# A gated group norm moved in among the state-space heads of a two-block transformer kernel

## The chip, the cores and the metric

One Trainium2 chip, one of its cores. The time is the device time of one execution of the whole program in microseconds. The kernel before took 2297.18 us (median of 3 runs, 2294.38 to 2307.04).

## The reference, cut to what matters

The program computes two blocks of two layers each over 256 tokens of width 1024, all in float32. The change is in the second block. One of its layers is, cut:

```python
h = rms_norm(x, norm1_w)
z, xbc, dt_raw, q, k, v = split(h @ w_in)          # z, x: 1024 wide; q: 1024; k, v: 256
xbc = silu(depthwise_conv_centered(xbc, conv_w, conv_b))
y_ssm = ssd_fwd + ssd_bwd + d_skip * xs             # 16 heads of 64, state-space
y_ssm = y_ssm * silu(z)                             # the gate
y_ssm = rms_norm(y_ssm in 2 groups of 512) * w      # one mean of squares per group and token
y_attn = windowed_gqa(q, k, v, sink, band_bias)     # 16 heads of 64
x = x + concat(y_ssm, y_attn) @ w_out
x = x + (silu(conv(h2 @ w_gate)) * (h2 @ w_up)) @ w_down
```

The mean of squares of a group needs all eight heads of that group, and nothing of the other.

## The kernel before

Activations lie transposed: 128 channels on the partitions, 256 tokens in the free dimension, so a width of 1024 is eight tiles of 128x256, and a pair of heads of 64 channels is one tile. Weights stream from memory in chunks of 1 MB through a ring of three (`raw2`). Float32 accuracy comes from splitting: ACT rounds a chunk to `w_hi` (L1664), DVE subtracts to get `w_lo` (L1382), and PE makes three products for each pair of tiles (L1451). So a chunk costs 48 matmuls on PE, two ACTIVATEs and two subtractions. The inputs are split the same way (`u_hi`, `u_lo`; `y_hi`, `y_lo`). Two chunks are held split at a time.

The order of the work is a list, `plan_second` (L1148). Each engine walks the list and issues its part of each step, in order; what crosses engines waits on a counting semaphore. At a chunk's step ACT and DVE first round and subtract the chunk of the next weighted step (`due`, L76), then deal with the step's own result. A step of PE that is held up therefore holds all that comes behind it on PE, and the same for ACT and DVE.

The steps around the change, for each layer:

- `xbc` (six chunks): convolution and silu on DVE and ACT (tanh, in the buffers `cth` and `cacc`).
- then ten chunks interleaved with 23 short steps: `ak2`, `av2`, `aq2` 0 to 3, `z` 0 to 3, in this order, among four `x_turn` and nineteen `ssd` steps. A chunk's projection takes PE about 5.9 us. A `z` chunk is followed by a tanh (L1736, ACT) and a product (L1899, DVE) that leaves 2 silu(z) in `zs`.
- `ssd` i, for the heads: PE spreads the decay of head i (L1600, L1601), DVE makes exponents of it (L1915), ACT takes the exponential (L1743), DVE multiplies by the masked product C B in the next step (L1922), PE multiplies by the tokens three steps later (L1608). After each pair of heads, at even i from 4 to 18, DVE adds the skip term and writes `yT` for that pair (L1926).
- `ssd_gate`: DVE multiplies all eight tiles of `yT` by `zs` and 0.5 in one instruction (L1931); ACT loads the table with log and exp and squares all (L1746, L1747).
- `att2` 0 and 1: the scores of attention heads 0 and 1.
- `ssd_norm`: PE sums the squares of both groups (L1616), ACT takes rsqrt as exp(-0.5 ln) (L1750, L1751), DVE scales eight tiles (L1939), ACT rounds them (L1754), DVE subtracts (L1945).
- `att2` 2 to 18, with the eight `wo2` chunks of the output projection between them. `att2` i holds on PE the scores of head i (L1511), values of head i-3 (L1532), and the turning of the probabilities of head i-2 (L1521); on DVE bias, maximum, division (L1957 to L1969) and the rest of the rounded output (L1976); on ACT two exponentials and two copies. `WO_AFTER` says after which `att2` each `wo2` comes. `wo2` 0 to 3 read `y_hi`, `y_lo`, two tiles each, and 4 to 7 the attention's output. All eight accumulate in the four banks `PB` (the trace's `projected`).
- `rms` 1 and the feed-forward.

Projections take the four `PB` banks in turn (`ROTATED2`, `turn`); scores use banks 0 and 1 of `MB` (`mixed`), turning bank 2, values bank 3, and the state-space pairs banks 2 and 3.

Of the kernel before, what the change touches and what calls it, by code (L numbers as in the profile page):

```python
# [27 lines left out]
P = 128  # L28
# [115 lines left out]
def first_block(nc, ctx, A, hT, k):  # L144
# [966 lines left out]
    with nc.Block() as block:  # L1111

        @block.gpsimd
        def _(pool):
# [24 lines left out]

WO_AFTER = (3, 5, 7, 9, 11, 13, 16, SH + VALUES - 1)  # L1140


COUNT2 = {"rms": 2, "dt": 1, "dt_rows": 1, "xbc": XBC // 2, "dt_columns": 1, "cb": 1, "ak2": 1, "av2": 1, "aq2": 4, "z": 4,
          "x_turn": 4, "ssd": SH + VALUES, "ssd_gate": 1, "att2": SH + VALUES, "ssd_norm": 1, "wo2": 8,
          "wg": FP, "wu": FP, "wd": FP, "add": 1}


def plan_second():  # L1148
    plan = [("rms", 0), ("dt", 0), ("xbc", 4), ("dt_rows", 0), ("xbc", 5), ("dt_columns", 0), ("xbc", 0), ("cb", 0)]
    plan += [("xbc", i) for i in range(1, 4)]  # L1150
    ssd = [("x_turn", i) for i in range(4)] + [("ssd", i) for i in range(SH + VALUES)]
    plan += interleave([("ak2", 0), ("av2", 0)] + [("aq2", i) for i in range(4)] + [("z", i) for i in range(4)], ssd)
    plan += [("ssd_gate", 0), ("att2", 0), ("att2", 1), ("ssd_norm", 0)]

    for i in range(2, SH + VALUES):
        plan += [("att2", i)]
        if i in WO_AFTER:
# [15 lines left out]
HELD2 = [("wd", FP * l + FP - 1) for l in range(DEPTH - 1)] + [("wo2", 8 * l + 7) for l in range(DEPTH)]  # L1173
ROTATED2 = [s for s in PLAN2 if s[0] in WEIGHTED2 and s[0] not in ("wo2", "wd")]
XBC_ORDER = [i for kind, i in plan_second() if kind == "xbc"]


def second_block(nc, ctx, A, hT, k):
# [43 lines left out]
    def place(name, shape, at, dtype=F32):  # L1222
        return nc.alloc_sbuf_tensor_at(name, shape, dtype, offset=area + at * KB)
# [21 lines left out]
    grs = place("grs", [P, SG, T], 8)  # L1245
    y_hi = place("y_hi", [P, KT, T], 10, F32R)
    y_lo = place("y_lo", [P, KT, T], 18, F32R)
    o_hi = place("o2_hi", [P, KT, T], 26, F32R)
# [139 lines left out]
    def taken(step):  # L1388

        kind, N, l, i = local(step)  # L1390
        if kind == "xbc":
            return s_zc, 6 * l + XBC_ORDER.index(i) + 1
        return {"ak2": (s_k, l + 1), "av2": (s_v, l + 1), "aq2": (s_q, N + 1), "z": (s_zs, N + 1),
                "wg": (s_zf, N + 1), "wu": (s_hf, N + 1)}[kind]
# [5 lines left out]
    with nc.Block() as block:  # L1400
# [30 lines left out]
        def _(pe):  # L1431
# [83 lines left out]
            def attention_turn(l, n):  # L1515
                U = SH * l + n
                pe.wait_ge(s_an, U + 1)
                if U:
                    pe.wait_ge(s_pt, U)
                for b in range(4):  # L1520
                    m = pe.transpose(MB[2][:, b * P:(b + 1) * P], S[:, n % ABUF, b // 2, b % 2 * P:(b % 2 + 1) * P], ident[:])  # L1521
                m.then_inc(s_at, 1)
# [13 lines left out]
            for step in PLAN2:  # L1536
# [54 lines left out]
                elif kind == "ssd":  # L1591
# [10 lines left out]
                    if i >= VALUES:  # L1602
# [8 lines left out]
                        m.then_inc(s_y, 1)  # L1611
                elif kind == "ssd_norm":
                    pe.wait_ge(s_ysq, l + 1)
                    for g in range(SG):
                        for n in range(4):
                            m = pe.matmul(PB[0][:, g * T:(g + 1) * T], ones_g[:], sq[:, 4 * g + n, :],  # L1616
                                          start=n == 0, stop=n == 3)
                    m.then_inc(s_yvar, 1)
# [9 lines left out]
                elif kind == "wo2":  # L1628
                    if i in (0, 2):
                        pe.wait_ge(s_yn, 2 * l + i // 2 + 1)  # L1630
                    if i >= 4:
# [11 lines left out]
        def _(act):  # L1643
# [22 lines left out]
            def halves(ap):  # L1666
                return ap.rearrange("p (a t) -> p a t", a=2)

            for step in PLAN2:
# [62 lines left out]
                elif kind == "z":  # L1732
                    b = result(step)
                    if N >= 2:
                        act.wait_ge(s_zs, N - 1)
# [4 lines left out]
                elif kind == "ssd":  # L1740
                    if i < SH:
                        act.wait_ge(s_ex, SH * l + i + 1)
                        act.activation(W[:, i % ABUF, :], W[:, i % ABUF, :], ACT.Exp).then_inc(s_ee, 1)  # L1743
                elif kind == "ssd_gate":
                    act.wait_ge(s_yg, l + 1)
                    act.preload_act_table_set(LOG_EXP)  # L1746
                    act.activation(sq[:], yT[:], ACT.Square).then_inc(s_ysq, 1)  # L1747
                elif kind == "ssd_norm":
                    act.wait_ge(s_yvar, l + 1)
                    link(act.activation(grs[:], halves(PB[0][:]), ACT.Ln, bias=eps[:, 0:1]))  # L1750
                    act.activation(grs[:], grs[:], ACT.Exp, scale=-0.5).then_inc(s_yrs, 1)  # L1751
# [37 lines left out]
        def _(dve):  # L1789
# [37 lines left out]
            for step in PLAN2:  # L1827
# [81 lines left out]
                elif kind == "ssd":  # L1909
# [13 lines left out]
                    if i > VALUES and i % 2 == 0:  # L1923
# [3 lines left out]
                                                 in1=MB[2 + pair % 2][:, 0:T], op0=ALU.mult, op1=ALU.add).then_inc(s_yT, 1)  # L1927
                elif kind == "ssd_gate":
                    dve.wait_ge(s_yT, KT * l + KT)
                    dve.wait_ge(s_zs, 4 * l + 4)  # L1930
                    dve.scalar_tensor_tensor(out=yT[:].rearrange("p a t -> p (a t)"), in0=zs[:].rearrange("p a t -> p (a t)"),  # L1931
                                             scalar=0.5, in1=yT[:].rearrange("p a t -> p (a t)"),
                                             op0=ALU.mult, op1=ALU.mult).then_inc(s_yg, 1)
                elif kind == "ssd_norm":
                    dve.wait_ge(s_yg, l + 1)
                    dve.wait_ge(s_yrs, l + 1)
                    for n in range(2):
                        for kt in range(4 * n, 4 * n + 4):
                            ins = dve.scalar_tensor_tensor(out=yT[:, kt, :], in0=yT[:, kt, :], scalar=column(l, V2_SN + kt),  # L1939
                                                           in1=grs[:, n, :], op0=ALU.mult, op1=ALU.mult)  # L1940
                        ins.then_inc(s_yf, 1)
                    for n in range(2):
                        quad = slice(4 * n, 4 * n + 4)
                        dve.wait_ge(s_yh, 2 * l + n + 1)
                        dve.tensor_tensor(y_lo[:, quad, :], yT[:, quad, :], y_hi[:, quad, :].bitcast(F32),  # L1945
                                          ALU.subtract).then_inc(s_yn, 1)
# [377 lines left out]
```

## Time and profile before

| | |
|---|---|
| runs | 2307.04, 2294.38, 2297.18 us |
| profiled execution | 2307.46 us, its span 2305.7 us |
| PE busy | 2057.5 us, 89% |
| DVE busy | 1556.6 us, 68% |
| ACT busy | 989.3 us, 43% |
| mean granted clock of PE | 0.949 |

The profile is of one execution. Busy time of an engine counts the time in which at least one of its instructions ran. The granted clock is the share of TensorE's full speed, 2.4 GHz, that the chip granted; at the lower level, 1.2 GHz, it is 0.5. A timeline row has the start, the duration, the engine and line, the operation, what it writes and reads, and in brackets how long the engine was idle before and what ended that. PE's matmuls overlap, so the start to start distance (some 0.12 us for 128x256) is what counts, and not the duration. A float32 matmul that isn't split leaves two records. For steps that stand in both layers the rows are those of the first; its heads run from 1403 to 1489 us and its attention to 1600 us, those of the second from 1889 to 1974 and to 2085 us.

### The profile page before, as it was taken

To read this page: it belongs to the slowest core of one execution; us is meant where nothing else is said; L and a number is where in the kernel's file an instruction comes from. 1 tells how busy PE (TensorE), PEld (TensorE's weight loads), DVE (VectorE), ACT (ScalarE), POOL (GpSimd) and SP (SyncE) were. 2 spreads that over 40 slices of the span, in tenths; PEclk is the share of its full clock that TensorE was granted. 3 is DMA by queue.
4 is the path that set the end of the run, shared out by engine and by line. 5 is a ranking of instruction groups with operands and counts; after the bars stand their busy time and mean duration, and the time that the engine had idled before them with its cause. 6 is when DMAs were issued, how large, how long until landed. Compare 5 with 4: busy or idle time off the path is not lost. (4 is left out here: it accounts for less than half of the span.)

```text
span 2305.7 us, 37153 instructions
## 1 busy us (share of the span) xinstructions
PE 2057.5 (89%) x15578; PEld 1927.2 (84%) x15578; DVE 1556.6 (68%) x2612; ACT 989.3 (43%) x1424; POOL 16.5 (1%) x36
## 2 busy tenths in 40 slices
PE   2799999999988999999999588987999789897996
PEld 1798888989988988899999567776999678687996
DVE  5687767677668876766755368765666588665664
ACT  1453355444444534544444224444444324444442
POOL 0000000000010000000000000000000000000000
PEclk7899999999999999999999889999999899899998
DMA  5455533548744554344555134211555232123551
GB/s 214 165 188 196 190 122 146 183 158 304 259 158 142 201 189 165 132 162 165 212 209 183 70 132 144 92 67 63 194 191 189 74 132 106 62 85 132 198 194 63
DMA packets 52627, 358.98 MB, mean 156 GB/s; under 512 B 6107, under 2 KB 8763, under 8 KB 9836
## 3 DMA queue, kind: packets, MB, share of 16 engines
q1 hardware_dynamic: 52268, 356.51, 43.3%
q8 instruction: 123, 2.02, 0.4%
q14 instruction: 44, 0.36, 0.0%
q10 hardware_dynamic: 192, 0.10, 0.0%
HBM read 355.40 MB, written 1.08 MB: 155 GB/s over the span
## 5 line engine op out<-in xcount | busy, mean ns | idle before, releaser
L362 DVE TENSOR_TENSOR w_lo<-raw,w_hi 128x1024 fp32r<-128x1024 f32 x340 | 410.0, 1229 | 242.9 <-ACT w_hi L637 241.4
L417 PE MATMUL projected<-u_hi,w_hi 128*128 128x256 f32 x1728 | 492.1, 285 | 46.3 <-DVE w_lo L362 38.3
L637 ACT ACTIVATE w_hi<-raw 128x1024 fp32r<-128x1024 f32 x340 | 351.8, 1054 | 386.8 <-PE projected L417 311.7
L417 PE MATMUL projected<-u_lo,w_hi 128*128 128x256 f32 x1728 | 485.7, 281 | 0.0
L417 PE MATMUL projected<-u_hi,w_lo 128*128 128x256 f32 x1728 | 485.1, 281 | 0.0
L417 PEld LDWEIGHTS projected<-u_hi,w_hi 128*128 128x128 f32 x1728 | 332.3, 192 | 53.8 <-DVE w_lo L362 39.2
L1382 DVE TENSOR_TENSOR w_lo<-raw,w_hi 128x1024 fp32r<-128x1024 f32 x204 | 246.0, 1223 | 143.7 <-ACT w_hi L1664 143.5
L417 PEld LDWEIGHTS projected<-u_lo,w_hi 128*128 128x128 f32 x1728 | 330.7, 191 | 0.3
L417 PEld LDWEIGHTS projected<-u_hi,w_lo 128*128 128x128 f32 x1728 | 330.4, 191 | 0.0
L1451 PE MATMUL projected<-u_hi,w_hi 128*128 128x256 f32 x992 | 281.4, 284 | 25.9 <-DVE w_lo L1382 25.9
L1451 PE MATMUL projected<-u_lo,w_hi 128*128 128x256 f32 x992 | 279.1, 281 | 0.0
L1451 PE MATMUL projected<-u_hi,w_lo 128*128 128x256 f32 x992 | 278.9, 281 | 0.0
L1664 ACT ACTIVATE w_hi<-raw 128x1024 fp32r<-128x1024 f32 x204 | 210.9, 1054 | 157.3 <-PE projected L1451 138.9
L1451 PEld LDWEIGHTS projected<-u_hi,w_hi 128*128 128x128 f32 x992 | 189.7, 191 | 32.7 <-issue 23.4
L1451 PEld LDWEIGHTS projected<-u_lo,w_hi 128*128 128x128 f32 x992 | 191.0, 193 | 0.0
L1451 PEld LDWEIGHTS projected<-u_hi,w_lo 128*128 128x128 f32 x992 | 189.1, 191 | 0.0
L417 PE MATMUL mixed<-hid_hi,w_hi 128*128 128x256 f32 x352 | 98.2, 279 | 1.0 <-DVE w_lo L362 1.0
L417 PE MATMUL mixed<-hid_lo,w_hi 128*128 128x256 f32 x352 | 98.0, 279 | 0.0
L417 PE MATMUL mixed<-hid_hi,w_lo 128*128 128x256 f32 x352 | 98.0, 279 | 0.0
L1451 PE MATMUL mixed<-hid_hi,w_hi 128*128 128x256 f32 x352 | 98.0, 278 | 0.0
L1451 PE MATMUL mixed<-hid_lo,w_hi 128*128 128x256 f32 x352 | 98.0, 278 | 0.0
L1451 PE MATMUL mixed<-hid_hi,w_lo 128*128 128x256 f32 x352 | 98.0, 278 | 0.0
(355 smaller groups left out, 4132.7 us busy)
## 6 DMA issues: line engine op xcount, KB each, us to landing
raw<-in_stream_dram SPq DMA_DIRECT2D x324, 1024.0 KB, 4.9
w_mod<-in_first_ada_dram SPq DMA_DIRECT2D x8, 1024.0 KB, 13.8
band<-bias_rows SPq DMA_DIRECT2D x1, 3072.0 KB, 13.0
x<-in_xT_dram SPq DMA_DIRECT2D x1, 1024.0 KB
out_dram<-f_sq SPq DMA_DIRECT2D x2, 512.0 KB, 2.6
tri<-in_tri_dram SPq DMA_DIRECT2D x2, 384.0 KB, 4.5
c<-in_c_dram SPq DMA_DIRECT2D x1, 512.0 KB
mask<-in_mask_dram SPq DMA_DIRECT2D x1, 384.0 KB, 3.8
```

Of the source, the lines that this page charges most:

```text
L362: eng.tensor_tensor(part(w_lo, step, half), raw_half(step, half), part(w_hi, step, half).bitcast(F32), ALU.subtract).then_inc(s_lo_pool if ...
L417: m = pe.matmul(out, a, b, start=start and n == 0, stop=stop and n == 2, **kw)
L637: act.activation(part(w_hi, step, half), raw_half(step, half), ACT.Copy).then_inc(s_hi, 1)
L1382: eng.tensor_tensor(part(w_lo, step, half), raw_half(step, half), part(w_hi, step, half).bitcast(F32), ALU.subtract).then_inc(s_lo_pool if ...
L1451: m = pe.matmul(out, a, b, start=start and n == 0, stop=stop and n == 2, **kw)
L1664: act.activation(part(w_hi, CHUNKS2[n], half), raw_half(CHUNKS2[n], half), ACT.Copy).then_inc(s_hi, 1)
```

## The change

- The norm's two parts become one step kind, `group_norm` 0 and 1, one for each group.
- Gate and square move into `ssd`, by pair: DVE gates the tile as soon as `yT` of the pair is there (even i from 4 to 18), ACT squares it in the same step.
- `group_norm` 0 stands behind `ssd` 11; its sum goes to a bank of the rotation. `group_norm` 1 stands behind `att2` 1, with its sum in `MB[2]`, the bank of the turned probabilities; the first turning waits until it was read. The table with log and exp is loaded in `group_norm` 0 only.
- Rounding and subtraction go by two tiles, with a count for each of the four `wo2` chunks that read them.
- The chunks among the heads come in the order `z` 0 to 3, `ak2`, `av2`, `aq2` 0 to 3. `z` 0 and 1 wait on ACT for the last convolution, whose buffers they use.
- `wo2` 0 comes behind `group_norm` 1, and `WO_AFTER` is (1, 3, 5, 7, 9, 12, 15, 18).
- `y_hi` lies over `zs` and `y_lo` over `yT`.

```diff
-WO_AFTER = (3, 5, 7, 9, 11, 13, 16, SH + VALUES - 1)
+WO_AFTER = (1, 3, 5, 7, 9, 12, 15, SH + VALUES - 1)
...
-    plan += interleave([("ak2", 0), ("av2", 0)] + [("aq2", i) for i in range(4)] + [("z", i) for i in range(4)], ssd)
-    plan += [("ssd_gate", 0), ("att2", 0), ("att2", 1), ("ssd_norm", 0)]
+    plan += interleave([("z", i) for i in range(4)] + [("ak2", 0), ("av2", 0)] + [("aq2", i) for i in range(4)], ssd)
+    plan.insert(plan.index(("ssd", 11)) + 1, ("group_norm", 0))
+    plan += [("att2", 0), ("att2", 1), ("group_norm", 1), ("wo2", 0)]
...
-    y_hi = place("y_hi", [P, KT, T], 10, F32R)
-    y_lo = place("y_lo", [P, KT, T], 18, F32R)
+    y_hi = place("y_hi", [P, KT, T], 58, F32R)
+    y_lo = place("y_lo", [P, KT, T], 50, F32R)
...
             def attention_turn(l, n):
                 U = SH * l + n
                 pe.wait_ge(s_an, U + 1)
+                if n == 0:
+                    pe.wait_ge(s_yrs, SG * l + SG)
...
-                elif kind == "ssd_norm":
-                    pe.wait_ge(s_ysq, l + 1)
-                    for g in range(SG):
-                        for n in range(4):
-                            m = pe.matmul(PB[0][:, g * T:(g + 1) * T], ones_g[:], sq[:, 4 * g + n, :],
-                                          start=n == 0, stop=n == 3)
+                elif kind == "group_norm":
+                    out = bank(step) if i == 0 else MB[2]
+                    pe.wait_ge(s_ysq, 4 * N + 4)
+                    for n in range(4):
+                        m = pe.matmul(out[:, 0:T], ones_g[:], sq[:, 4 * i + n, :], start=n == 0, stop=n == 3)
                     m.then_inc(s_yvar, 1)
...
-                    if i in (0, 2):
-                        pe.wait_ge(s_yn, 2 * l + i // 2 + 1)
+                    if i < 4:
+                        pe.wait_ge(s_yn, 4 * l + i + 1)
...
                 elif kind == "z":
                     b = result(step)
+                    if i < 2:
+                        act.wait_ge(s_xbc, 6 * l + 6)
...
-                elif kind == "ssd_gate":
-                    act.wait_ge(s_yg, l + 1)
-                    act.preload_act_table_set(LOG_EXP)
-                    act.activation(sq[:], yT[:], ACT.Square).then_inc(s_ysq, 1)
...
+                    if i > VALUES and i % 2 == 0:
+                        pair = (i - 4) // 2
+                        act.wait_ge(s_yg, KT * l + pair + 1)
+                        act.activation(sq[:, pair, :], yT[:, pair, :], ACT.Square).then_inc(s_ysq, 1)
+                elif kind == "group_norm":
+                    act.wait_ge(s_yvar, N + 1)
+                    if i == 0:
+                        act.preload_act_table_set(LOG_EXP)
+                    out = PB[turn(step)] if i == 0 else MB[2]
+                    link(act.activation(grs[:, i, :], out[:, 0:T], ACT.Ln, bias=eps[:, 0:1]))
+                    act.activation(grs[:, i, :], grs[:, i, :], ACT.Exp, scale=-0.5).then_inc(s_yrs, 1)
                     for n in range(2):
-                        act.wait_ge(s_yf, 2 * l + n + 1)
-                        act.activation(y_hi[:, 4 * n:4 * n + 4, :], yT[:, 4 * n:4 * n + 4, :], ACT.Copy)\
-                           .then_inc(s_yh, 1)
+                        pair = slice(4 * i + 2 * n, 4 * i + 2 * n + 2)
+                        act.wait_ge(s_yf, 2 * N + n + 1)
+                        act.activation(y_hi[:, pair, :], yT[:, pair, :], ACT.Copy).then_inc(s_yh, 1)
...
-                elif kind == "ssd_gate":
-                    dve.wait_ge(s_yT, KT * l + KT)
-                    dve.wait_ge(s_zs, 4 * l + 4)
-                    dve.scalar_tensor_tensor(out=yT[:].rearrange("p a t -> p (a t)"), in0=zs[:].rearrange("p a t -> p (a t)"),
-                                             scalar=0.5, in1=yT[:].rearrange("p a t -> p (a t)"),
-                                             op0=ALU.mult, op1=ALU.mult).then_inc(s_yg, 1)
...
+                        dve.wait_ge(s_yT, KT * l + pair + 1)
+                        dve.wait_ge(s_zs, 4 * l + pair // 2 + 1)
+                        dve.scalar_tensor_tensor(out=yT[:, pair, :], in0=zs[:, pair, :], scalar=0.5, in1=yT[:, pair, :],
+                                                 op0=ALU.mult, op1=ALU.mult).then_inc(s_yg, 1)
```

On DVE `group_norm` i scales the four tiles of its group (two by two), and subtracts them two by two, each counted in `s_yn`.

## Rows read from the trace of the kernel before

**Rows 1.** The page, part 1: busy us, share of the span, instructions of each engine.

```profile
PE 2057.5 (89%) x15578; PEld 1927.2 (84%) x15578; DVE 1556.6 (68%) x2612; ACT 989.3 (43%) x1424; POOL 16.5 (1%) x36
```

**Rows 2.** Stretches: length, busy us of each engine, granted clock, DMA share, GB/s.

```profile
1489.00:1524.90 35.90, 25.08 (x129) 20.54 (x129) 24.50 (x59) 16.07 (x37) 0.00 (x0) 0.81 0.11 38
1974.00:2009.60 35.60, 24.78 (x129) 20.33 (x129) 24.50 (x59) 16.06 (x37) 0.00 (x0) 0.81 0.11 38
1524.90:1536.40 11.50, 10.85 (x84) 9.39 (x82) 7.86 (x22) 5.51 (x15) 0.00 (x0) 1.00 0.27 93
1427.50:1489.00 61.50, 61.37 (x423) 49.31 (x422) 47.62 (x85) 25.74 (x31) 0.00 (x0) 1.00 0.29 100
```

**Rows 3.** Waits of PE from 1489.0 to 1524.9: us, times, longest.

```profile
PE mixed L1532 <- ACT PT L1763: 3.7, 1, 3.7
```

**Rows 4.** Timeline of PE, 1489 to 1525: start, duration, line, what; idle before.

```profile
1489.60 1.14 PE L1511 MATMUL mixed<-kT,qT 64*128 64x256 f32 x8 [0.57 <-DVE yT L1926]
...
1495.15 5.41 PE L1616 MATMUL projected<-sq,ones_m 128*128 128x256 f32 x16 [4.41 <-ACT sq L1747]
...
1511.17 0.56 PE L1451 MATMUL projected<-y_hi,w_hi 128*128 128x256 f32 x1
...
1524.91 0.37 PE L1451 MATMUL projected<-y_hi,w_hi 128*128 128x256 f32 x1
```

**Rows 5.** Timeline of DVE, 1489 to 1511.

```profile
1489.58 2.29 DVE L1931 SCALAR_TENSOR_TENSOR yT<-zs,yT 128x2048 f32<-128x2048 f32 x1
1491.79 0.68 DVE L1957 TENSOR_TENSOR S<-mixed,band 128x512 f32<-128x512 f32 x1
...
1493.57 0.68 DVE L1957 TENSOR_TENSOR S<-mixed,band 128x512 f32<-128x512 f32 x1
...
1502.04 3.26 DVE L1939 SCALAR_TENSOR_TENSOR yT<-yT,vec,grs 128x256 f32<-128x256 f32 x8 [4.83 <-ACT grs L1751]
...
1507.57 0.68 DVE L1957 TENSOR_TENSOR S<-mixed,band 128x512 f32<-128x512 f32 x1
...
1510.27 0.68 DVE L1957 TENSOR_TENSOR S<-mixed,band 128x512 f32<-128x512 f32 x1
```

**Rows 6.** Timeline of ACT, the same stretch.

```profile
1491.89 1.28 ACT L1746 ACT_TABLE_LOAD   x1 [6.02 <-DVE yT L1931]
1493.18 1.91 ACT L1747 ACTIVATE sq<-yT 128x2048 f32<-128x2048 f32 x1
1495.00 0.19 ACT L1772 ACTIVATE es<-es 128x2 f32<-128x2 f32 x1
...
1496.08 0.19 ACT L1772 ACTIVATE es<-es 128x2 f32<-128x2 f32 x1
```

**Rows 7.** Timeline of DVE among the state-space heads.

```profile
1435.47 1.39 DVE L1915 TENSOR_SCALAR W<-mixed,cols 128x256 f32<-128x256 f32 x4 [1.83 <-PE mixed L1608]
...
1453.63 0.69 DVE L1899 SCALAR_TENSOR_TENSOR zs<-cth,projected 128x512 f32<-128x512 f32 x1 [0.52 <-ACT cth L1736]
1455.17 1.39 DVE L1915 TENSOR_SCALAR W<-mixed,cols 128x256 f32<-128x256 f32 x4 [0.85 <-PE mixed L1608]
```

**Rows 8.** Groups by line and shape, 1386 to 1625: busy us, mean ns | idle before.

```profile
L1939 DVE SCALAR_TENSOR_TENSOR yT<-yT,vec,grs 128x256 f32<-128x256 f32 x8 | 3.3, 481 | 4.8 <-ACT grs L1751 4.8
...
L1684 ACT ACTIVATE rstd<-lnv 128x256 f32<-128x256 f32 x1 | 0.4, 416 | 0.0
...
L1542 PE MATMUL mixed<-sqn,ones_d 128*128 128x256 f32 x16 | 3.7, 386 | 1.4 <-ACT sqn L1679 1.4
```

**Rows 9.** Stretches with their clock, and PE's row after a long idle.

```profile
1594.60:1600.40 5.80, 5.71 (x48) 5.51 (x48) 0.03 (x1) 0.81 (x1) 0.00 (x0) 1.00 0.00 0
1511.10:1519.20 8.10, 8.10 (x51) 7.97 (x51) 4.18 (x10) 3.68 (x8) 0.00 (x0) 0.71 0.17 43
...
1878.00:1885.00 7.00, 6.97 (x48) 6.93 (x48) 6.42 (x15) 0.55 (x2) 0.00 (x0) 0.79 0.44 150
...
1878.03 0.55 PE L1451 MATMUL projected<-u_hi,w_hi 128*128 128x256 f32 x1 [4.27 <-DVE w_lo L1382]
```

More of the change, by code:

```diff
@@ L1137 @@
 V2_END = V2_SINK + AH
-WO_AFTER = (3, 5, 7, 9, 11, 13, 16, SH + VALUES - 1)
+WO_AFTER = (1, 3, 5, 7, 9, 12, 15, SH + VALUES - 1)
 COUNT2 = {"rms": 2, "dt": 1, "dt_rows": 1, "xbc": XBC // 2, "dt_columns": 1, "cb": 1, "ak2": 1, "av2": 1, "aq2": 4, "z": 4,
-          "x_turn": 4, "ssd": SH + VALUES, "ssd_gate": 1, "att2": SH + VALUES, "ssd_norm": 1, "wo2": 8,
+          "x_turn": 4, "ssd": SH + VALUES, "group_norm": 2, "att2": SH + VALUES, "wo2": 8,
           "wg": FP, "wu": FP, "wd": FP, "add": 1}
@@ L1173 @@
 HELD2 = [("wd", FP * l + FP - 1) for l in range(DEPTH - 1)] + [("wo2", 8 * l + 7) for l in range(DEPTH)]
-ROTATED2 = [s for s in PLAN2 if s[0] in WEIGHTED2 and s[0] not in ("wo2", "wd")]
+ROTATED2 = [s for s in PLAN2 if s[0] in WEIGHTED2 and s[0] not in ("wo2", "wd") or s[0] == "group_norm" and s[1] % SG == 0]
 XBC_ORDER = [i for kind, i in plan_second() if kind == "xbc"]
@@ L1392, in taken @@
             return s_zc, 6 * l + XBC_ORDER.index(i) + 1
-        return {"ak2": (s_k, l + 1), "av2": (s_v, l + 1), "aq2": (s_q, N + 1), "z": (s_zs, N + 1),
+        return {"group_norm": (s_yrs, N + 1), "ak2": (s_k, l + 1), "av2": (s_v, l + 1), "aq2": (s_q, N + 1), "z": (s_zs, N + 1),
                 "wg": (s_zf, N + 1), "wu": (s_hf, N + 1)}[kind]
@@ L1743, in _ @@
                         act.activation(W[:, i % ABUF, :], W[:, i % ABUF, :], ACT.Exp).then_inc(s_ee, 1)
-                elif kind == "ssd_gate":
-                    act.wait_ge(s_yg, l + 1)
-                    act.preload_act_table_set(LOG_EXP)
-                    act.activation(sq[:], yT[:], ACT.Square).then_inc(s_ysq, 1)
[L1748 to L1751, printed above, removed]
+                    if i > VALUES and i % 2 == 0:
[9 more added lines that the diff above has]
+                    act.activation(grs[:, i, :], grs[:, i, :], ACT.Exp, scale=-0.5).then_inc(s_yrs, 1)
                     for n in range(2):
-                        act.wait_ge(s_yf, 2 * l + n + 1)
-                        act.activation(y_hi[:, 4 * n:4 * n + 4, :], yT[:, 4 * n:4 * n + 4, :], ACT.Copy)\
-                           .then_inc(s_yh, 1)
+                        pair = slice(4 * i + 2 * n, 4 * i + 2 * n + 2)
+                        act.wait_ge(s_yf, 2 * N + n + 1)
+                        act.activation(y_hi[:, pair, :], yT[:, pair, :], ACT.Copy).then_inc(s_yh, 1)
                 elif kind == "att2":
@@ L1927, in _ @@
                                                  in1=MB[2 + pair % 2][:, 0:T], op0=ALU.mult, op1=ALU.add).then_inc(s_yT, 1)
-                elif kind == "ssd_gate":
-                    dve.wait_ge(s_yT, KT * l + KT)
-                    dve.wait_ge(s_zs, 4 * l + 4)
-                    dve.scalar_tensor_tensor(out=yT[:].rearrange("p a t -> p (a t)"), in0=zs[:].rearrange("p a t -> p (a t)"),
-                                             scalar=0.5, in1=yT[:].rearrange("p a t -> p (a t)"),
-                                             op0=ALU.mult, op1=ALU.mult).then_inc(s_yg, 1)
-                elif kind == "ssd_norm":
-                    dve.wait_ge(s_yg, l + 1)
-                    dve.wait_ge(s_yrs, l + 1)
+                        dve.wait_ge(s_yT, KT * l + pair + 1)
+                        dve.wait_ge(s_zs, 4 * l + pair // 2 + 1)
+                        dve.scalar_tensor_tensor(out=yT[:, pair, :], in0=zs[:, pair, :], scalar=0.5, in1=yT[:, pair, :],
+                                                 op0=ALU.mult, op1=ALU.mult).then_inc(s_yg, 1)
+                elif kind == "group_norm":
+                    dve.wait_ge(s_yg, 4 * N + 4)
+                    dve.wait_ge(s_yrs, N + 1)
                     for n in range(2):
-                        for kt in range(4 * n, 4 * n + 4):
+                        for kt in range(4 * i + 2 * n, 4 * i + 2 * n + 2):
                             ins = dve.scalar_tensor_tensor(out=yT[:, kt, :], in0=yT[:, kt, :], scalar=column(l, V2_SN + kt),
-                                                           in1=grs[:, n, :], op0=ALU.mult, op1=ALU.mult)
+                                                           in1=grs[:, i, :], op0=ALU.mult, op1=ALU.mult)
                         ins.then_inc(s_yf, 1)
                     for n in range(2):
-                        quad = slice(4 * n, 4 * n + 4)
-                        dve.wait_ge(s_yh, 2 * l + n + 1)
-                        dve.tensor_tensor(y_lo[:, quad, :], yT[:, quad, :], y_hi[:, quad, :].bitcast(F32),
+                        pair = slice(4 * i + 2 * n, 4 * i + 2 * n + 2)
+                        dve.wait_ge(s_yh, 2 * N + n + 1)
+                        dve.tensor_tensor(y_lo[:, pair, :], yT[:, pair, :], y_hi[:, pair, :].bitcast(F32),
                                           ALU.subtract).then_inc(s_yn, 1)
```

## The prediction

> **What bounds the kernel now.** I read the busy table first: PE is busy 89% of the span, DVE 68% [rows 1]. So an edit pays where PE stands idle, or where it closes a gap after which PE runs slow. The windows by stage say where that is. Among the state-space heads PE is busy for 61.37 of 61.50 us at clock 1.00. From 1489.0 to 1524.9, where the heads end, the norm runs and the attention starts, it is busy for 25.08 of 35.90 us at clock 0.81; the second layer repeats it with 24.78 of 35.60 [rows 2]. The reader should see in these four lines that the change aims at the one stage of its neighbourhood in which PE waits.
>
> The timelines tell why. PE has issued the scores of two attention heads at 1489.60 and then waits 4.41 us for the squares [rows 4]: DVE gates all eight tiles in one 2.29 us instruction [rows 5], then ACT loads a table (1.28) and squares all of them (1.91) [rows 6]. PE sums the squares in 5.41 us, at the low clock. DVE cannot start to normalise before 1502.04, and holds the third score block until 1507.57 [rows 5], for which PE waits 3.7 us with the attention [rows 3]. wo2 0 starts at 1511.17, wo2 1 at 1524.91 [rows 4]. wo2 0 takes 8.0 us at clock 0.71, where a chunk of 48 matmuls at clock 1.00 takes 5.71 [rows 9]. Idle is 35.90 - 25.08 = 10.8 us; the low clock costs 2.3 there and 5.41 - 3.72 = 1.7 in the sum of squares, going by the equal sum of 16 at L1542 [rows 8]. Together 14.8 us per layer is to be had.
>
> From wo2 1 on, the section runs in periods of 11.5 us: one wo2 chunk (5.7) and two attention heads (5.8), of which PE is busy 10.85 [rows 2]. There DVE has 3.6 us to spare per period.
>
> **The heads, with z first.** z 0 and z 1 take the places of ak2 and av2. The weights are of one size, 1 MB each, in the same ring, so SP's queue is as before. z 1 may start on its first half, where av2 waited for both; that gives PE about 1.2 us, but DVE now has four z products of 0.69 [rows 7] among x_turn and the first heads, and the first values product already waits for DVE there. I take +0.3 us (bounds -1.2 and +1.5). ACT's new wait of z 0 for the last convolution is met before its weights are rounded; queued behind it are the roundings for z 2, which PE wants 6 us later.
>
> **Gate and square by pair.** Each of eight pairs gets a gate on DVE, by the same shape 0.48 [rows 8] (2.29 in one piece goes), and a square on ACT of 0.42, going by an ACTIVATE of that size [rows 8]. Behind each square on ACT stands the rounding of the next chunk, and behind that DVE's subtraction: with the handovers it all comes 1.4 us later per pair. DVE now waits for PE after it, 1.83 us before an ordinary pair [rows 7], so it fits. In the later pairs the slack is only 0.85, but a z product (0.69 and the 0.52 waited for it) stood there and is gone [rows 7]. Cost on PE 0; if the cover fails, up to 0.5 per pair. The end of the heads: gate and square of pair 7 are 1.0 us after the last product instead of 6.1.
>
> **First group's norm among the heads.** PE goes into group_norm 0 right behind step 11. The gate of pair 3 ends on DVE about 1.2 us after PE is there, the square 0.5 later: a wait of 1.75 us, where behind it on PE stands the projection aq2 1, and for that all of ACT and DVE. Then 4 matmuls, half of 3.72 [rows 8]: 1.86. The rest lies beside the projection: table load 1.28 [rows 6], Ln and Exp 0.47 and 0.42, two pairs scaled (4 x 0.41 from 3.26 for 8 [rows 5]), rounded and subtracted, some 5.3 us in all. ACT's rounding for aq2 2 comes 5.5 us later than now and DVE is through with it some 8 us after the projection began; PE wants it after 10 (5.9 of projection, 4.2 of two heads). So the cover holds by about 2 us. Lower bound of the whole step: 1.9, the matmuls alone; upper: 1.9 + 4.4, the wait for squares as it is now [rows 4].
>
> So the heads end 0.3 + 1.75 + 1.86 = 3.9 us later, less 0.1 for the z product that stood before the last head: 3.8.
>
> **From the last head to wo2 1**, counted from the end of the last values product. Scores of two heads 0.6 to 1.7, as now. Squares are ready at 1.5, sum of the second group 1.75 to 3.6. wo2 0 follows at once, as the first group is long normalised: 3.6 to 9.3, at full clock, and its weights were rounded before. In this time DVE and ACT do the rest. DVE: scores 0 and 1 take 1.78 each [rows 5], from 1.6 to 5.2, the division of head 0 until 6.2. ACT: exponentials, 1.1 per head [rows 6], until 6.4, then Ln and Exp until 7.4. DVE scales, ACT rounds, DVE subtracts until 10.4; the weights of wo2 1 are rounded and subtracted by 13.1 (2.36 on DVE). Then DVE takes score block 2 and the division of head 1, 2.7 together [rows 5]: 15.9. PE meanwhile runs scores 2, turn 0, scores 3, values 0 until 13.4 and waits 2.6 us for turn 1. The new wait of turn 0 for the group's reciprocal root was met at 7.4. wo2 1 starts at 16.4.
>
> Now it starts at 35.9 [rows 2], but behind two more heads, worth 5.8; so the gain is 35.9 - 16.4 - 5.8 = 13.7. Less 3.8: 9.9 us. For the second layer, with 35.6, it is 9.6.
>
> **Rest of the attention.** wo2 5 and 6 stand behind groups of three heads, and three heads are left before wo2 7. PE's stalls of 0.65 per odd head: one fewer in the middle, one of 1.4 instead of 0.7 at the end. Taken as 0 (bounds -0.5, +1.5 per layer).
>
> Sum: 9.9 + 9.6 = 19.5 us. The profiled execution took 2307.46 us (span 2305.7) and would take 2288.0. Its time lies above the median of the three runs, 2297.18; from this I get 2277.7.
>
> **The clock in the new gaps.** After 4.27 us without a matmul the stretch 1878 to 1885 has clock 0.79 [rows 9]. The Trainium skill ("TensorE: Matmul & The Clock Gate", section "HAM oscillation — how this bites in real kernels") says that a loop whose bursts are separated by waits goes back to half rate each time and pays for warming up each time. By it the 2.6 us wait ahead of turn 1 would hand wo2 1 the price that wo2 0 has now; the trace has an idle stretch only longer than this one to show for it.
>
> On the table load the Trainium skill ("ScalarE: Activation LUTs", section "What ACT_TABLE_LOAD costs") adds a drain to the load, 2.66 us in all. The row differs: the Square starts 0.01 us after the 1.28 us load [rows 6]. By the page group_norm 0 would end 1.4 us later, and most of the 2 us of cover would be gone.
>
> **Rivals.**
> 1. The clock falls in the gap at turn 1 (or the gaps around group_norm 0 come longer). Mechanism in rows: 2.3 us for a slow chunk of wo2 [rows 9], and 1.5 more of waiting at group_norm 0. Per layer 9.8 - 3.8 = 6.0, so -12: 2285. For it: 4.27 us of idle do it, and DVE's chain in the attention is long. Against: 2.6 is much shorter. Chance 0.20.
> 2. More is closed than I count: the wait at turn 1 vanishes because the weights are rounded earlier, and group_norm 0 finds its squares ready. Then 9.8 + 2.6 + 1.75 = 14.1 per layer, -28: 2269. For: the full 14.8 is what the rows offer. Against: DVE's order is fixed. Chance 0.12.
> 3. No gain: with wo2 earlier, the attention is paced by its own DVE and ACT chain, and what PE saves ahead it waits for later. It takes 1.4 us on each of seven periods. Against: 3.6 us of DVE slack per period [rows 2]. Time 2297. Chance 0.08.
> 4. Slower: the pair's chain (gate, square in front of the rounding on ACT, rounding, subtraction) delays the next head's exponents beyond the slack, in every pair. Place: DVE's first instruction of a pair; from 1.83 us of delay on it costs PE one for one [rows 7]. To pay back 9.8 per layer it must overshoot by 1.4 on each of seven pairs; at 4 us of chain, it overshoots by 2.2, 15 per layer against 9.8: +11, 2308. Against: 0.48 and 0.42 are measured shapes. Chance 0.04.
> That the edit does not do what it says would be wo2 0 waiting all the same, since it needs squares of pair 3 through y_lo; they are 30 us old by then, so I leave it out.
>
> **Numbers.** My forecast has 0.56. A measurement of this kernel tells 0.5% (11.5 us) from no change. Rival 1 lies at this edge; three quarters of it count as faster. Faster 0.56 + 0.12 + 0.14 = 0.82, same 0.14, slower 0.04. The forecast alone spans 2271 to 2284 (2 to 3 us each way per layer). The range takes in rivals 1 and 2 and the spread of the medians: 2266 to 2290.
>
> **What would show it.** The stretch from the last L1608 to the second wo2 chunk, 35.9 now, should be 16 to 17 us. The sum of squares should appear twice per layer, 8 records each; PE's wait before the first 1 to 2.5 us. wo2 0 should take 5.7 us at clock 1.00. PE in the heads should have no wait but that one. The table load should stand among the heads. The prediction is wrong if PE waits for W or w_lo among the heads in several pairs, if PE waits over 4 us at turn 1, or if the period after wo2 1 exceeds 11.5.

## The result and the profile after

The changed kernel takes 2285.28 us (median of 7 runs, 2277.00 to 2292.26), the kernel before 2300.94 us on the same chips (7 runs, 2294.38 to 2308.85). The ratio is 0.9925, with a 95% interval from 0.9897 to 0.9952, so 17 us are gained, with an uncertainty of 6. The profiled execution took 2287.97 us.

```profile
span 2286.2 us, 37218 instructions
...
PE 2045.6 (89%) x15578; PEld 1918.2 (84%) x15578; DVE 1558.6 (68%) x2630; ACT 993.1 (43%) x1446; POOL 16.5 (1%) x36
```

PE is busy for 12 us less than before in the first part of the page, with the same 15578 matmuls [rows 1]. Of these, 7.6 us lie in the stages that the change touches (4.1 and 3.5, by windows): there slow matmuls have gone as well as gaps. The rest comes from stretches in which both kernels have the same code.

The windows of the first layer after: the heads, from the first x_turn to the end of the last values product (PE's product of the last head with its tokens, L1611); from there to wo2 1; and wo2 1 itself (columns as in [rows 2]).

```profile
1397.80:1488.10 90.30, 87.30 (x616) 72.29 (x616) 74.47 (x132) 44.91 (x60) 0.00 (x0) 1.00 0.32 110
1488.10:1504.50 16.40, 12.76 (x89) 10.81 (x89) 13.57 (x34) 8.40 (x23) 0.00 (x0) 1.00 0.23 84
1504.50:1511.80 7.30, 7.30 (x51) 7.17 (x49) 4.38 (x11) 3.68 (x8) 0.00 (x0) 0.77 0.23 65
```

The 35.9 us of [rows 2] have become 16.4, at clock 1.00, and PE is busy in 12.76 of them. But wo2 1 runs at clock 0.77. The timeline of PE, same layer:

```profile
1457.53 0.89 PE L1619 MATMUL projected<-sq,ones_m 128*128 128x256 f32 x3 [1.79 <-ACT sq L1751]
...
1488.65 1.14 PE L1512 MATMUL mixed<-kT,qT 64*128 64x256 f32 x8 [0.57 <-DVE yT L1933]
1489.73 1.99 PE L1619 MATMUL mixed<-sq,ones_m 128*128 128x256 f32 x8
1491.37 0.47 PE L1452 MATMUL projected<-y_hi,w_hi 128*128 128x256 f32 x1
...
1500.38 1.09 PE L1535 MATMUL mixed<-PT,vA 128*64 128x128 f32 x8 [0.50 <-ACT PT L1770]
1504.05 0.66 PE L1524 MATMUL mixed<-ident,S 128*128 128x128 f32 x4 [2.58 <-DVE S L1974]
1504.46 0.37 PE L1452 MATMUL projected<-y_hi,w_hi 128*128 128x256 f32 x1
...
1511.71 0.48 PE L1512 MATMUL mixed<-kT,qT 64*128 64x256 f32 x1
```

The answers to [rows 4], in order: the first sum stands among the heads with a wait of 1.79 us; the second follows the scores at once and wo2 0 follows it at 1491.37, 3.3 us after the last values product (22.2 before). Ahead of turn 1, the turning of the probabilities of head 1, PE waits 2.58 us, and wo2 1 then takes 7.3 us. DVE's timeline says why PE waits:

```profile
1488.63 0.42 DVE L1937 SCALAR_TENSOR_TENSOR yT<-zs,yT 128x256 f32<-128x256 f32 x1
1489.82 0.69 DVE L1962 TENSOR_TENSOR S<-mixed,band 128x512 f32<-128x512 f32 x1 [0.76 <-PE mixed L1512]
...
1495.61 1.67 DVE L1944 SCALAR_TENSOR_TENSOR yT<-yT,vec,grs 128x256 f32<-128x256 f32 x4 [1.21 <-ACT grs L1758]
1497.20 1.47 DVE L1950 TENSOR_TENSOR y_lo<-yT,y_hi 128x512 fp32r<-128x512 f32 x2
1498.92 2.36 DVE L1383 TENSOR_TENSOR w_lo<-raw,w_hi 128x1024 fp32r<-128x1024 f32 x2 [0.25 <-ACT w_hi L1666]
1501.20 0.68 DVE L1962 TENSOR_TENSOR S<-mixed,band 128x512 f32<-128x512 f32 x1
...
1503.37 0.62 DVE L1974 TENSOR_SCALAR S<-S,den 128x256 f32<-128x256 f32 x2
```

Scores, then the second group's scaling (1495.61) and subtraction (1497.20), the weights of wo2 1 (1498.92), and only then score block 2 (1501.20) and the division of head 1 (1503.37), done at 1503.99. Turn 1 follows at 1504.05. Among the heads, ACT has the first group's norm:

```profile
1456.97 0.42 ACT L1751 ACTIVATE sq<-yT 128x256 f32<-128x256 f32 x1 [0.88 <-DVE yT L1937]
...
1459.52 1.28 ACT L1755 ACT_TABLE_LOAD   x1 [0.40 <-PE projected L1619]
1460.82 0.47 ACT L1757 ACTIVATE grs<-projected,eps 128x256 f32<-128x256 f32 x1
1461.32 0.42 ACT L1758 ACTIVATE grs<-grs 128x256 f32<-128x256 f32 x1
```

For a ledger I measure one stage in each layer: from the first x_turn matmul to the end of wo2 7. It took 198.9 and 199.0 us before and 189.9 and 190.7 after: 17.3 us together, which is the measured gain. The spans of the two profiles differ by 19.5 us. The rest comes from stretches with the same code: up to the first x_turn the profile of after is 3.7 us shorter, between the two stages 1.9 longer, behind the second 0.4 shorter.

### The profile page after: what moved, and what is told of

Its sections match the earlier page's. It is cut to its first block and busy times, and to the rows that moved or that the text cites. A ratio compares the mean times of both kernels' runs of the same rounds, so it can differ in the third digit from the quotient of the medians.

```text
span 2286.2 us, 37218 instructions
## 1 busy us (share of the span) xinstructions
PE 2045.6 (89%) x15578; PEld 1918.2 (84%) x15578; DVE 1558.6 (68%) x2630; ACT 993.1 (43%) x1446; POOL 16.5 (1%) x36
## 5 line engine op out<-in xcount | busy, mean ns | idle before, releaser
L1452 PE MATMUL projected<-u_hi,w_hi 128*128 128x256 f32 x992 | 282.3, 285 | 26.4 <-DVE w_lo L1383 26.4
```

The lines of the kernel that those rows point to most:

```text
L1452: m = pe.matmul(out, a, b, start=start and n == 0, stop=stop and n == 2, **kw)
```

## Experiments

Starts of wo2 chunks are counted from the end of the last values product; "stage" is the stretch of the ledger, in the first and the second layer. Each kernel was profiled once and the changed one twice. The ratios to before have intervals of 6 to 10 us to either side, more than most steps between neighbours. So the steps are read from the stages and the waits in them; the ratios show a gain against before from the third kernel on, and little order among the kernels.

**A ladder from before to after.** The first three kernels go from one to the other in steps; the fourth takes the early group away from the full change.

*z first alone*: the kernel before, with

```diff
-    plan += interleave([("ak2", 0), ("av2", 0)] + [("aq2", i) ...] + [("z", i) ...], ssd)
+    plan += interleave([("z", i) ...] + [("ak2", 0), ("av2", 0)] + [("aq2", i) ...], ssd)
```

and the wait of the first two z chunks.

> The kernel before with one edit: z chunks first, ak2, av2 and aq2 behind them. Measured on the stage from the first x_turn matmul to the last wo2 matmul: before 198.9 and 199.0 us in the two layers, after the change 189.9 and 190.7. My theory: the gain comes from PE's waits around the norm, which this edit leaves alone; it only takes the z product from in front of the last head (0.6 to 1.0 us). Stage 198 us, run 1 to 3 us below before. Rival (the order of the chunks is what helps, since gate and table load no longer collide with tanh): stage 194 or less, run 8 us or more below before.

Measured: stage 199.0 and 198.8; 2300.48 us, ratio to before 1.0011 (0.9982 to 1.0041). The first values product comes 0.9 us earlier, the last only 0.4 to 0.6, and wo2 0 0.3 later after it. The order of the chunks gives nothing by itself that these numbers show; the 1 us that I expected was too much.

*Gate and square by pair, norms at the end*: the change without

```diff
-    plan.insert(plan.index(("ssd", 11)) + 1, ("group_norm", 0))
-    plan += [("att2", 0), ("att2", 1), ("group_norm", 1), ("wo2", 0)]
+    plan += [("att2", 0), ("att2", 1), ("group_norm", 0), ("group_norm", 1)]
```

and with the old WO_AFTER.

> The change with both group norms behind att2 1 and the wo2 chunks at their old places (after att2 3, 5, 7, 9, 11, 13, 16, 18): so z first and gate and square by pair, nothing else. My theory: the squares are ready 1.5 us after the last values product instead of 6.1, but the table load and both groups' scaling still stand ahead of the third score block; wo2 0 starts about 18 us after the last values product (22.1 before), stage about 194. Rival (early gates and squares are the whole gain): wo2 0 at 12 or less, stage 190 as after.

Measured: heads 87.1 and 86.9 (87.2 and 87.0 with z first alone), wo2 0 starts at 18.8, stage 195.4 and 195.1 (I expected 194); ratio 0.9975 (0.9943 to 1.0008). PE has no wait for the last head's product here. PE's waits in the 36 us behind the last values product (us, times, longest) have one large entry, the reciprocal root of the second group, for which the bank of the turning is held:

```profile
PE mixed L1523 <- ACT grs L1757: 5.8, 1, 5.8
```

*First group among the heads, wo2 at the old places*: the change with the old WO_AFTER and no wo2 0 behind group_norm 1.

```diff
-WO_AFTER = (1, 3, 5, 7, 9, 12, 15, SH + VALUES - 1)
+WO_AFTER = (3, 5, 7, 9, 11, 13, 16, SH + VALUES - 1)
-    plan += [("att2", 0), ("att2", 1), ("group_norm", 1), ("wo2", 0)]
+    plan += [("att2", 0), ("att2", 1), ("group_norm", 1)]
```

> The change with the wo2 chunks at their old places only; the first group's norm is among the heads. My theory: wo2 0 starts 13.6 us after the last values product (DVE has one group less ahead of the attention), but the heads take 3.6 us longer, so the stage is about 193, 1 us better than without the early group, and 3 us worse than the full change, since PE has nothing to fill the wait for DVE. Rival (the early first group is what brings the gain): stage 190, as after. The other rival (it costs more in the heads than it gives): stage 195 or more.

Measured: wo2 0 at 14.1, heads 90.5 and 90.2, stage 192.9 and 192.9; ratio 0.9959 (0.9930 to 0.9989). The early group is worth 2.6 and 2.2 us at this step, where I had expected 1. The same wait has halved, and wo2 0 behind it takes 7.1 us instead of 8.1:

```profile
PE mixed L1524 <- ACT grs L1758: 2.8, 1, 2.8
```

*Norms late, wo2 0 right behind*: the full change but for group_norm 0, which stands just ahead of group_norm 1.

```diff
-    plan.insert(plan.index(("ssd", 11)) + 1, ("group_norm", 0))
-    plan += [("att2", 0), ("att2", 1), ("group_norm", 1), ("wo2", 0)]
+    plan += [("att2", 0), ("att2", 1), ("group_norm", 0), ("group_norm", 1), ("wo2", 0)]
```

> The change with group_norm 0 moved from behind ssd 11 to just ahead of group_norm 1, wo2 0 still right behind. My theory: the heads get 3.6 us shorter, wo2 0 starts at about 11 us after the last values product instead of 3.3 and at the low clock, wo2 1 at 21 to 22.5 instead of 16.4; stage 192 to 193, 2.5 us per layer worse than the change. Rival (the wait and the sum inside the heads cost as much as they bring): stage 190, same as after. If the early group were the main thing, the stage would be 195 or more.

Measured: heads 87.5 and 87.1, wo2 0 at 11.3, wo2 1 at 23.8, stage 193.0 and 192.7; ratio 0.9944 (0.9916 to 0.9973). That is 3.1 and 2.0 worse than the change; wo2 1 comes later than the 21 to 22.5 that I expected. Now PE waits ahead of wo2 0, for the first group's rest:

```profile
PE projected L1451 <- DVE y_lo L1949: 5.9, 1, 5.9
```

So in the first layer: 0.1 lost by the order, 3.5 gained by gating and squaring in pairs, 2.6 by the early group, 3.0 by wo2 0 in the gap and the other new places of wo2. In the second: 0.2, 3.7, 2.2 and 2.2 gained. And the early group, once wo2 0 fills the gap, is worth 3.1 and 2.0. No single part is the change. I had expected 1, 4, 1 and 3.

**The waits that are left.** Each of the next kernels takes one wait out of the changed kernel. The recorded expectations call them n1 to n6.

*First norm one projection later* (n1): group_norm 0 behind ssd 13.

```diff
-    plan.insert(plan.index(("ssd", 11)) + 1, ("group_norm", 0))
+    plan.insert(plan.index(("ssd", 13)) + 1, ("group_norm", 0))
```

> The change with group_norm 0 behind ssd 13 instead of ssd 11, so one projection later on PE. My theory: PE's 1.8 us wait for the squares of pair 3 is a matter of place only; it goes, and nothing takes its stead: stage 188.1 and 188.9 (after: 189.9 and 190.7), run 3 to 4 us below after. Rival (ACT and DVE are too late for the last chunk then, as the norm's 5 us chain now stands nearer to the end of the heads): PE waits for w_lo or W among the last heads and the stage stays at 190.

Measured: stage 190.4 and 190.7, not shorter; ratio 0.9901 (0.9869 to 0.9934). The wait for the squares is gone, and another stands in its place, 1.0 us (1.4 in the second layer) for DVE's product of the last head (L1611; PE's waits in the heads):

```profile
PE mixed L1592 <- DVE xbc L1891: 1.1, 1, 1.1
PE mixed L1611 <- DVE W L1929: 1.0, 1, 1.0
PE mixed L1603 <- DVE W L1922: 0.8, 1, 0.8
```

So the rival holds, for 1.0 and 1.4 of the missing 1.8 us. The rest lies in chunks that took 5.9 to 6.0 us where they took 5.7 to 5.8 in the profile of after, with no wait in them (see the last section).

*Second group scaled later* (n2): scaling, rounding and subtraction of group_norm 1 become a step of their own behind att2 3.

```diff
+        if i == 3:
+            plan += [("group_scale", 0)]
```

> The change with the second group's scaling, rounding and subtraction (3 us on DVE) taken out of group_norm 1 and put behind att2 3; the sum, Ln and Exp stay. My theory: PE's 2.6 us wait for turn 1 is DVE's queue, in which the second group stands in front of score block 2; it goes, and with it the low clock in which wo2 1 took 7.3 us instead of 5.7: wo2 1 starts 13.7 us after the last values product (16.4 in after) and takes 5.7; stage 4.2 shorter, 185.7 and 186.5, run 8 us below after. Rival (the attention's own chain of scores, exponentials and division is the limit there): wait for turn 1 stays above 1.5, stage 188 or more. Rival on the clock (the low clock of wo2 1 has nothing to do with the wait): wo2 1 still takes 7.3.

Measured: wo2 1 at 13.95 in both layers (16.38), stage 187.0 and 189.2, where I expected 185.7 and 186.5; ratio 0.9882 (0.9837 to 0.9926). Timelines of DVE and then of PE:

```profile
1495.54 0.68 DVE L1968 TENSOR_TENSOR S<-mixed,band 128x512 f32<-128x512 f32 x1
...
1497.71 0.62 DVE L1980 TENSOR_SCALAR S<-S,den 128x256 f32<-128x256 f32 x2
...
1500.94 1.67 DVE L1950 SCALAR_TENSOR_TENSOR yT<-yT,vec,grs 128x256 f32<-128x256 f32 x4
1502.53 1.47 DVE L1956 TENSOR_TENSOR y_lo<-yT,y_hi 128x512 fp32r<-128x512 f32 x2
1504.26 2.36 DVE L1385 TENSOR_TENSOR w_lo<-raw,w_hi 128x1024 fp32r<-128x1024 f32 x2 [0.26 <-ACT w_hi L1668]
1506.54 0.68 DVE L1968 TENSOR_TENSOR S<-mixed,band 128x512 f32<-128x512 f32 x1
...
1498.38 0.65 PE L1526 MATMUL mixed<-ident,S 128*128 128x128 f32 x4 [0.52 <-DVE S L1980]
...
1509.80 1.06 PE L1537 MATMUL mixed<-PT,vA 128*64 128x128 f32 x8 [1.59 <-DVE o_lo L1987]
```

and the window of wo2 1:

```profile
1498.80:1504.40 5.60, 5.60 (x51) 5.49 (x48) 5.07 (x16) 4.19 (x10) 0.00 (x0) 1.00 0.16 69
```

The wait ahead of turn 1 is 0.52, wo2 1 takes 5.7 us at clock 1.00. So the wait was DVE's queue, and the low clock came with the wait: both rivals fall. The other profiles bear it out. With 2.58 us ahead of turn 1 (the change, its second execution, the kernels with the norm behind ssd 13 and with the tail edit) wo2 1 takes 7.3 to 7.4 us, in all eight cases; with 0.5 to 0.7 (this kernel and the last three) 5.7 to 5.9, in all eight. But 1.59 us are now waited for o_lo where the changed kernel waits 0.65: the scaling stands in front of score block 4 instead. wo2 2 starts 3.1 us earlier, not 4.2. In the second layer the last chunk, wo2 7, took 7.32 us instead of 5.73, at the low clock, behind waits no longer than in the other profiles (see the last section).

*Tail* (n3): wo2 6 one place later.

```diff
-WO_AFTER = (1, 3, 5, 7, 9, 12, 15, SH + VALUES - 1)
+WO_AFTER = (1, 3, 5, 7, 9, 12, 16, SH + VALUES - 1)
```

> The change with wo2 6 behind att2 16 instead of 15. My theory: the 1.5 us wait ahead of the values of head 14 gets covered by the chunk again: stage 0.8 us shorter, run 1.6 below after, hard to see in the time. Rival: the stall moves and the stage stays.

Measured: wo2 7 starts at 93.4 and 93.3 (93.9 and 94.1), stage 189.6 and 189.2; ratio 0.9902 (0.9864 to 0.9940). The stall of 1.5 us is gone, and 0.5 to 0.8 us of it is to be seen at wo2 7. In the stage it is 0.3 and 1.5, as the heads differ from profile to profile too.

*All three* (n4): the edits of n1, n2 and n3 together.

```diff
-WO_AFTER = (1, 3, 5, 7, 9, 12, 15, SH + VALUES - 1)
+WO_AFTER = (1, 3, 5, 7, 9, 12, 16, SH + VALUES - 1)
-    plan.insert(plan.index(("ssd", 11)) + 1, ("group_norm", 0))
+    plan.insert(plan.index(("ssd", 13)) + 1, ("group_norm", 0))
+        if i == 3:
+            plan += [("group_scale", 0)]
```

> The three edits of n1, n2 and n3 together. If they are independent waits on PE, the stage is 1.8 + 4.2 + 0.8 = 6.8 us shorter than after in each layer: 183.1 and 183.9, run about 13.5 us below after and 31 below before. If one of them only uncovers another wait, it is less: the rival says that DVE becomes the limit between the last head and wo2 1, and gives 186 or more.

Measured: stage 186.3 and 186.7, ratio 0.9861 (0.9823 to 0.9898). The three waits are not independent: 3 us of the expected 6.8 are missing. What is there is the gain of the second and third edit; the first gives nothing again, with a wait of 1.0 and 1.4 us for the last head's product. The rival has the number right but not the place: wo2 1 starts at 13.96 as with the second edit alone.

**Two better places, and the change once more.** The changed kernel ran again beside the two:

> The changed kernel itself, unedited, beside the two versions below. What repeats in a second execution is the kernel's, and what doesn't is the chip's. My theory: wo2 0 and wo2 1 start 3.3 and 16.4 us after the last values product again, wo2 1 takes 7.2 to 7.3 us, the wait ahead of the first sum is 1.8, and the stage from x_turn to wo2 7 is within 1 us of 190.3. The feed-forward, whose code the change leaves alone, took 195.5 us in some profiles and 202 to 203 in others with no wait of PE in either; it will be one of these two. Rival: the stage differs by 2 us or more, and then the terms of my sum cannot be read from single profiles.

Measured: wo2 0 at 3.29 and wo2 1 at 16.38 and 16.39, a wait of 1.78 for the first sum, 2.58 for turn 1, wo2 1 7.32 and 7.42 us; stage 190.7 and 190.8; ratio 0.9906 (0.9879 to 0.9933). The waits repeat to 0.01 us, the stage to 0.8, and the first feed-forward took 196.2 us where it had taken 203.4.

*Behind a projection* (n5, against the kernel with all three):

```diff
-    plan.insert(plan.index(("ssd", 13)) + 1, ("group_norm", 0))
+    plan.insert(plan.index(("aq2", 1)) + 1, ("group_norm", 0))
```

> The scaling after att2 3 and wo2 6 behind att2 16 as in n4, but group_norm 0 straight behind the projection aq2 1 instead of behind ssd 13. In n1, behind ssd 13, PE's wait for the squares was gone and 1.0 us of waiting for the products of DVE had come at the end of the heads. My theory: that was the chain of 5 us standing too near the end; 4.2 us earlier it is covered at both ends: no wait at the sum, none but the 0.6 before the attention at the end, stage 184.6 to 185.6 (n4: 186.3 and 186.7), as 1.8 is saved against the change instead of 0.8. Rival (DVE's total among the heads is what lacks, wherever the norm stands): a wait of about 1 us turns up at the end or at a values product again, stage 186 or more.

Measured: stage 186.4 and 187.1, ratio 0.9874 (0.9844 to 0.9904), as the rival has it. No wait at the sum, and the one at the end is there as before (1.15, in the second layer 1.52). PE:

```profile
1464.78 1.89 PE L1621 MATMUL projected<-sq,ones_m 128*128 128x256 f32 x8
...
1490.09 0.86 PE L1613 MATMUL mixed<-W,xtok_fwd 128*64 128x256 f32 x4 [1.15 <-DVE W L1933]
```

DVE ahead of it:

```profile
1482.71 0.47 DVE L1937 SCALAR_TENSOR_TENSOR yT<-xbc,vec,mixed 128x256 f32<-128x256 f32 x1
1483.22 0.42 DVE L1941 SCALAR_TENSOR_TENSOR yT<-zs,yT 128x256 f32<-128x256 f32 x1
1483.56 1.38 DVE L1926 TENSOR_SCALAR W<-mixed,cols 128x256 f32<-128x256 f32 x4
...
1486.81 2.36 DVE L1385 TENSOR_TENSOR w_lo<-raw,w_hi 128x1024 fp32r<-128x1024 f32 x2 [0.99 <-ACT w_hi L1668]
1489.09 0.95 DVE L1933 TENSOR_TENSOR W<-W,cbm 128x768 f32<-128x768 f32 x1
```

Here my theory falls: in both places DVE comes to the last head's product (1489.09) only behind its last weights (1486.81), and those stand behind pair 5's two instructions, 0.9 us of them, and ACT's square and rounding. In the changed kernel PE comes 1.0 us later to the same place (1.9 in the second layer) and finds the product done, by 0.06 and 0.3 us. So the wait for the squares cost less than it looked, because a wait of over 1 us stood behind it. Gate and square alone don't make that wait: with the norms late (the second and fourth kernel of the ladder) the same instructions stand there and PE doesn't wait for the last product. It comes only with the first group's norm among the heads, which gives DVE 3.1 us of scaling and subtraction and PE a sum of 1.6. And it is the heads as a whole that don't yield: in all nine profiles with the early group they take 90.2 to 90.9 us, in whichever of the three places it stands. That DVE's total sets this is argued from these numbers, and no run takes work off DVE there.

*Scaling in two halves*, behind att2 3 and 4 (n6, against the kernel with the norm behind a projection):

```diff
+        if i in (3, 4):
+            plan += [("group_scale", i - 3)]
```

> As n5, but the second group is scaled in two parts, a pair after att2 3 and a pair after att2 4. In n2 and n4 PE's wait at turn 1 was gone, and 1.4 to 1.6 us of waiting for o_lo had come after wo2 1, where the changed kernel waits 0.65: DVE's queue, one step later. My theory: with half the scaling in front of score block 4 this wait falls to about 0.7, stage 0.8 shorter than n5, run 1 to 2 us. Rival (DVE is short of time between the heads and wo2 2 as a whole): the wait moves to wo2 2, which needs both pairs, and the stage stays.

Measured: the wait for o_lo is 0.80, wo2 2 starts at 25.6 (26.4), stage 185.6 and 185.3, so 0.7 and 1.8 shorter, as expected or better; 2271.02 us (6 runs), ratio to before 0.9864 (0.9836 to 0.9893); the changed kernel beside it took 2279.23 us. The wait of 1.15 at the last head is still there. By the stage this is the version to keep: it is 13.2 and 13.7 us shorter than before, where the change gives 9.0 and 8.3. By the time alone it can't be told from the kernel with all three edits (ratio 0.9861).

## Why the prediction was right

The time came out 17.3 us below before by the ratio, against 19.5, and where the gain was to come from is where it came from. The time itself, 2285.28 us, is 7.6 above the forecast of 2277.7 and outside the 2271 to 2284 that the forecast alone spans; it lies in the range because the range takes in rival 1 and the spread of the medians. Half of the 7.6 (3.8) is that the kernel before has 2300.94 over seven runs, where I had 2297.18 from three. That the profiled execution took 2287.97 where I had 2288.0 is luck: 2.2 of the 19.5 us between the two profiles lie in stretches with the same code. Part of the sum is luck too: in the first layer the clock took 1.6 us that I had left out and the rest of the attention 0.4, and the heads gave back 1.05.

- **The gap** (35.9 to 16.4 by the working): 16.38, in both layers and in two executions. Each item stands in the trace where the working had it, the squares 1.4 us after the last product, DVE's order, turn 1 at the end.
- **The heads** (3.8 longer): 2.75 and 3.3. The wait was 1.79 against 1.75, the sum 1.6 instead of 1.86, and z first gave 0.4 to 0.6 where I charged 0.3. The wait for the squares is not the only one, as I had said it would be: with z first PE waits 0.8 us at the first heads for DVE's W, and the 1.4 us for w_lo that stood ahead of them are down to 0.3. The cover of 2 us behind the first sum was 1.6: the weights of aq2 2 were ready at 1467.53, and PE took them at 1469.08.
- **Gate and square cost PE nothing**: true, by the ladder. The heads take 87.1 and 86.9 us with them and 87.2 and 87.0 without (z first alone). The reason I gave covers the pairs; I did not look at the last head, where DVE's product was done 0.6 us before PE wanted it without them and 0.3 with them. There the work of the early group is felt as soon as the norm stands at another place (1.0 to 1.5 us, norm behind ssd 13 or behind aq2 1), and in the changed kernel it was hidden behind the wait for the squares. It has something of my fourth rival, at one place instead of seven and not through gate and square alone.
- **The clock**, in the first rival with 2.3 us per layer: it happened, behind a gap of 2.58 us, with 1.6 (7.32 against 5.71; in the second layer 1.4, against 5.90). The half of rival 1 on more waiting at group_norm 0 did not happen. This is the largest term that the forecast lacked, and my reason against it, that 2.6 us is much shorter than 4.27, was wrong. The kernel with the second group scaled later shows the wait as the cause: with 0.5 instead of 2.6 us of waiting the chunk takes 5.7. The trace agrees in kind with what the Trainium skill says ("TensorE: Matmul & The Clock Gate", section "HAM oscillation — how this bites in real kernels"), a burst behind a wait that starts at half rate; the waits of its example are longer than 2.58 us, so by it alone the term could not be sized. The 1.79 us gap among the heads left the projection behind it at 5.8 and 6.0.
- **Rest of the attention as 0**: 0.4 us lost, the stall of 1.5 at the values of head 14 (the tail experiment).
- **Table load**: Ln starts 0.02 us after the load of 1.28 (1459.52 and 1460.82 above). The drain that the Trainium skill adds ("ScalarE: Activation LUTs", section "What ACT_TABLE_LOAD costs") is not to be seen; the measurement decides.
- **The chances**: three quarters of rival 1's 0.20 are 0.15, and not the 0.14 that I added up.

First layer: -13.7 (the gap, two heads deducted) + 2.75 + 1.6 + 0.4 = -8.95, which is the stage's difference. The rivals "no gain" and "slower" are refuted by the period behind wo2 2, 11.47 us as before, and by the waits among the heads, of which none stands behind a pair's gate and square. As for the second rival, its 14.1 us per layer are nearly to be had, but by another order of DVE's work: the last kernel gets 13.2 and 13.7.

## What to carry to other kernels

Walk the instruction queues of all engines item by item through a gap that is to be closed: the order on DVE decided here to 0.1 us what remained. After it, look at who stands just behind the wait that you remove, since a second, shorter wait can be hidden there. And give a gap of PE that is left a second price, that of a slow chunk behind it: here 2.58 us of waiting cost 1.4 to 1.6 more.

## What the runs showed of the hardware

**PE has two paces at the same granted clock.** In windows of 50 us with PE busy throughout, in the first feed-forward, the kernel before and the one with z first (same instructions there) had:

```profile
1700.00:1750.00 50.00, 50.00 (x427) 50.00 (x426) 31.73 (x42) 23.45 (x27) 0.00 (x0) 1.00 0.54 187
```

```profile
1700.00:1750.00 50.00, 50.00 (x444) 50.00 (x443) 33.40 (x46) 24.58 (x28) 0.00 (x0) 1.00 0.54 192
```

427 against 444 matmuls, clock 1.00 in both, so 117 or 113 ns per 128x256 matmul. Both paces turn up in one kernel: among the heads a projection takes 5.73 or 5.93 us, in the same profile, and the first feed-forward took 195 to 196 us in eight of the thirteen profiles and 202 to 203 in the others. At 7 us in each of two feed-forwards that is of the size by which runs of one kernel differ (15 us over 7 runs of the change, 27 over 31 runs of before), and it is why a stage's waits, which repeat to 0.01 us, tell more than its length. What sets it was not tried.

**PE's clock behind its waits**, for the chunks of the stages, by the longest wait since the chunk before: with 2.6 to 2.8 us the chunk took 7.1 to 7.4, with 4.4 to 5.9 it took 7.8 to 8.2, with 1.8 and less 5.7 to 6.0. There is one exception: wo2 7 in the second layer of the kernel with the second group scaled later. Its rows on PE, and its window:

```profile
2039.88 1.06 PE L1537 MATMUL mixed<-PT,vA 128*64 128x128 f32 x8 [1.51 <-DVE o_lo L1987]
2042.21 1.09 PE L1537 MATMUL mixed<-PT,vA 128*64 128x128 f32 x8 [0.69 <-ACT PT L1774]
2044.23 0.38 PE L1454 MATMUL projected<-o_hi,w_hi 128*128 128x256 f32 x1 [0.93 <-DVE o_lo L1987]
```

```profile
2044.20:2051.60 7.40, 7.32 (x48) 7.13 (x48) 0.01 (x1) 0.82 (x1) 0.00 (x0) 0.77 0.00 0
```

The same three waits stand ahead of wo2 7 in the first layer of that profile, where it took 5.73. So the length of a wait alone doesn't settle the clock of the next chunk; what else does was not tried.
